# The recurrence's input projection of a two-block transformer: one plain weight slot on raw input, seven slots with seven products each, gates and scan at fixed points

## What is computed

```
x = rmsnorm(x, final_g)                       # end of the first block
h = rms_norm(x, a_norm)                       # a second norm right behind it
proj = h @ w_in                               # 1024 -> 2048
y_branch, x_branch = jnp.split(proj, 2, axis=-1)
gate = gelu(y_branch)                         # tanh form
xc = causal_depthwise_conv(x_branch, conv_w, conv_b)        # 4 taps
r_gate, i_gate = sigmoid(xc by blocks @ w_a + b_a), sigmoid(xc by blocks @ w_x + b_x)
log_a = -8 * r_gate * softplus(-lam)
a, u = exp(log_a), sqrt(-expm1(2 * log_a)) * (i_gate * xc)
h_t = a_t * h_{t-1} + u_t                     # a scan over the 512 positions
x = x + (gate * h) @ w_out                    # the stage called YA
x = x + swiglu(rms_norm(x, a_ffn_norm))       # the stage called SW0
```

## Time and profile before

| | |
|---|---|
| median of 3 runs | 3285.03 us (3284.56 to 3289.19) |
| span of the profiled execution | 3286.2 us |
| PE busy | 3255.1 us, 99% |
| VectorE busy | 2027.2 us, 62% |
| ScalarE busy | 730.0 us, 22% |
| GpSimd busy | 1028.5 us, 31% |
| granted TensorE clock, mean | 0.997 of full speed |

### The profile page before, as it was taken

The page is one execution under the profiler, slowest core; times in us unless marked ns, Lnnn a source line. Parts: engine busy times, 40 slices in busy tenths (PEclk is TensorE's granted clock), DMA queues, the critical chain, the costliest instruction groups (busy, mean ns, idle before and its releaser), DMA issues. The chain is left out here.

```text
span 3286.2 us, 40354 instructions
## 1 busy us (share of the span) xinstructions
PE 3255.1 (99%) x15522; PEld 2464.8 (75%) x15522; DVE 2027.2 (62%) x3686; ACT 730.0 (22%) x1567; POOL 1028.5 (31%) x806
## 2 busy tenths in 40 slices
PE   8999999999999999999999999999999999999999
PEld 6767775555555566788888854888886887888888
DVE  8766777676765624278545656756536688866543
ACT  3432422010101333131111124211101235321111
POOL 0111323323232010224444401444441453344443
PEclk9999999999999999999999999999999999999999
DMA  6434412333331121332222221222223221122222
GB/s 261 138 102 128 126 52 79 114 122 110 119 107 55 61 88 49 97 87 78 90 90 90 80 87 64 80 88 90 90 90 101 81 82 53 40 77 90 90 90 90
DMA packets 66896, 304.51 MB, mean 93 GB/s; under 512 B 8496, under 2 KB 21168, under 8 KB 40720
## 3 DMA queue, kind: packets, MB, share of 16 engines
q1 hardware_dynamic: 54368, 268.68, 24.3%
q0 software_dynamic: 6528, 18.75, 1.8%
q10 hardware_dynamic: 5808, 14.49, 1.3%
HBM read 292.84 MB, written 2.88 MB: 90 GB/s over the span
## 5 line engine op out<-in xcount | busy, mean ns | idle before, releaser
L2857 POOL TENSOR_TENSOR scratch<-ring 128x512 f32<-128x512 f32 (+1 forms) x160 | 217.1, 1357 | 1443.6 <-PE psum L744 952.9
L744 PE MATMUL psum<-big,scratch 128*128 128x256 f32 (+1 forms) x2240 | 606.9, 426 | 0.0
L744 PEld LDWEIGHTS psum<-big,scratch 128*128 128x128 f32 x2240 | 425.6, 190 | 163.7
L744 PE MATMUL psum<-H,scratch 128*128 128x256 f32 (+1 forms) x2144 | 498.9, 387 | 0.0
L744 PEld LDWEIGHTS psum<-H,scratch 128*128 128x128 f32 x2144 | 406.5, 190 | 77.0 <-issue 5.0
L744 PE MATMUL psum<-big,ring 128*128 128x256 f32 (+1 forms) x1584 | 421.4, 418 | 6.6 <-DVE cb L2172 2.5
L744 PE MATMUL psum<-H,ring 128*128 128x256 f32 (+1 forms) x1536 | 396.2, 400 | 1.7 <-issue 0.7
L744 PEld LDWEIGHTS psum<-big,ring 128*128 128x128 f32 x1584 | 300.1, 190 | 111.9 <-DVE cb L2172 3.7
L1480 ACT ACTIVATE cb<-psum 128x256 f32<-128x256 f32 x336 | 129.0, 384 | 1011.0 <-PE psum L744 1011.0
L744 PEld LDWEIGHTS psum<-H,ring 128*128 128x128 f32 x1536 | 290.0, 190 | 76.8 <-ACT H L1578 6.4
L713 PE MATMUL psum<-H,ring 128*128 128x512 f32 x736 | 328.6, 598 | 0.0
(11 more groups left out here) (397 smaller groups left out, 4144.6 us busy)
## 6 DMA issues: line engine op xcount, KB each, us to landing
ring<-in_wall SPq DMA_DIRECT2D x202, 1024.0 KB, 4.9
big<-in_wada SPq DMA_DIRECT2D x48, 512.0 KB, 3.5
big<-in_wada POOLq DMA_DIRECT2D x32, 512.0 KB, 4.1
big<-in_wada SPq DMA_DIRECT2D x8, 1024.0 KB, 21.1
scratch<-in_rpb ACTq DMA_DIRECT2D x16, 512.0 KB, 4.0
big<-big ACTq DMA_DIRECT2D x64, 64.0 KB, 4.9
X<-in_xin SPq DMA_DIRECT2D x4, 768.0 KB, 6.9
scratch<-negd SPq DMA_DIRECT2D x8, 384.0 KB, 9.1
```

What stands on the lines that cost most here:

```text
L744: mm = pe.matmul(fast_bank(st, q, b), lhsT, rhs(k), start=start and k == 0, stop=k == kt - 1, skip_group_check=True)
L2857: pool.tensor_tensor(s1, a21, a22, ALU.add).then_inc(combo_own, 1)
```

## The change

1. The projection's eight plain slots become one plain slot (`raw_slot`) and a fast stage `RX` of seven slots of the new kind `"lru"`.
2. The plain slot's input is `X` times `g_sq` without the roots, written by ScalarE into `GT` as soon as the last MLP has left each tile. The sums of norm 4 (`token_sums`) stand behind its fourth matmul, the spreading of the roots (`spread_roots`) behind its eighth. Its two results are multiplied by the roots afterwards (`scale_first` on VectorE). The filler matmuls of norm 4 are gone (`BRIDGE` has no 4).
3. VectorE makes the input's combinations for `RX` (16 subtractions), interleaved with the first tiles' work, and three additions out of PSUM for each of the seven slots; ScalarE has three more copies and one quarter in each slot. GpSimd makes seven more sets of weight combinations; the first of them starts when slot 101 has landed.
4. The gates, the square roots, the scans, the gelu and the scaling of `X` stand at fixed points of the fast slots, on every engine. The conv's first tap moves from reading PSUM to reading `XB`.
5. The last tiles' gelu stands between the first and second group of `YA`'s input combinations, and in `YA`'s first slot product 2 comes after product 5.
6. `T2` moves to other memory, and a few semaphores are shared, with no other effect on the order.

Of the two functions `branches(x, n)` the first is ScalarE's and the second VectorE's; n is the place in the slot at which it is called.

```diff
-N_UNITS = 2 * 28 + 16 + 12
+N_UNITS = 2 * 28 + 2 + 12
...
+        if self.kind == "lru":
+            return [("lru", 0, s) for s in range(7)]
...
+RX = Stage("lru", False, 101, 72, 4, 0, 40, -1, 2, 8)
...
-                    elif q >= 2:
-                        pe.wait_ge(c21_done, q if rotated else q - 1)
+                    elif q >= 2:
+                        pe.wait_ge(c21_done, q if rotated or at_start(x) else q - 1)
...
-                    late = st.kind == "relu" and slots[x][0] == "out" and slots[x][2] == 0
+                    late = st.kind == "relu" and slots[x][0] == "out" and slots[x][2] == 0 or st is YA and x == 0
...
-            BRIDGE = {1: (3, 11), 2: (3, 12), 3: (3, 8), 4: (8, 5), 6: (4, 4)}
+            BRIDGE = {1: (3, 11), 2: (3, 12), 3: (3, 8), 6: (4, 4)}
...
-            norm(4)
+            def raw_slot():
+
+                r = wait_slot()
+                pe.wait_ge(c11_done, w.fast - 1)
+                pe.wait_ge(c21_done, w.fast - 1)
+                for f in range(2):
+                    for k in range(DT):
+                        if f == 0:
+                            pe.wait_ge(h_ready, 32 + k + 1)
+                        mm = pe.matmul(acc(w.unit), slot_cols(r, k, f * P, P), GT[:, k, :], start=k == 0, stop=k == 7)
+                        if f == 0 and k == 3:
+                            token_sums(4)
+                    mm.then_inc(half_done, 1)
+                    w.unit += 1
+                    if f == 0:
+                        spread_roots(4)
+                w.slot += 1
...
-            for s in range(8):
-                project(xq, normed=32 if s == 0 else None,
-                        after=lambda f, s=s: lru_gates(2 * s + f - 1) if 1 <= 2 * s + f <= DT else None)
-            for p in range(2):
-                pe.wait_ge(acc_free[p], w.unit // 2)
+            gates_at = {(0, 7): 0, (0, 4): 1, (1, 2): 2, (1, 6): 3, (2, 2): 4, (2, 6): 5, (3, 2): 6, (3, 6): 7}
+
+            def between_branches(x, i):
+                if (x, i) in gates_at:
+                    lru_gates(gates_at[x, i])
+
+            fast_stage(RX, between=between_branches)
...
+                    hook(x, 0)
                     copy(q, 5)
                     copy(q, 6)
+                    hook(x, 1)
...
+            def branches(x, n):
+                i = 2 * x + 2
+                y = i - DT
+                if n == 0:
...
+                    else:
+                        gelu_tanh(y - 1)
...
+                def to_branch(q, s):
+
+                    between(s, 0)
+                    took(2, q, c11_done, branch_half(s, 0, 0), 1)
+                    between(s, 1)
+                    took(3, q, c12_done, branch_half(s, 0, 1), 6)
+                    between(s, 2)
+                    took(7, q, c22_done, branch_half(s, 1, 1), 5)
+                    between(s, 3)
...
+            def branches(x, n):     
+
+                i, y = 2 * x + 2, 2 * x - 6
+                if n == 0:
+                    if 1 <= x < 4:
+                        conv(i - 1)
...
+                    if x > 3:
+                        gelu_cube(y - 1)
+                elif n == 1:
...
+                    if x > 3:
+                        lru_scan(y)
+                        gated(y - 1)
+                elif n == 2:
+                    if x > 3:
+                        lru_scan(y + 1)
+                else:
+                    if x < 3:
+                        conv(i)
...
+                    if x >= 3:
+                        gelu_cube(y)
+                    if x == 3:
+                        lru_input(7)
+                        lru_scan(1)
+                    if x in (4, 5):
+                        final_norm(2 * x - 4)
+                        final_norm(2 * x - 3)
+                    if x >= 3:
+                        gated(y)
...
-            pool.wait_ge(lru_v, DT)
+            mix_weights(RX)
             mix_weights(YA)
```

More of the change, by code:

```diff
@@ L287, in build @@
         consts_in = sem("consts_in")
-        x_in = [sem(f"x_in{g}") for g in range(4)]
         bias_in = [sem(f"bias_in{b}") for b in range(4)]
@@ L323, in build @@
         w_in = [sem(f"w_in{b}") for b in range(4)]
-        qw_in = [sem(f"qw_in{b}") for b in range(4)]
+        x_and_qw_in = [sem(f"input_and_query_weights_in{b}") for b in range(4)]
         kv_turned = sem("kv_turned")
@@ L733, in fast_stage, with at_start @@
                 rotated = st is HEADS
+                def at_start(x):
+                    return st is RX and x == 0
                 def product(x, i, b, cols, rhs, start, ready=None):
@@ L779, in first @@
                     elif q >= 2:
-                        pe.wait_ge(c21_done, q if rotated else q - 1)
+                        pe.wait_ge(c21_done, q if rotated or at_start(x) else q - 1)
+                    if st is RX and x == 1:
+                        for p in range(2):
+                            pe.wait_ge(acc_free[p], w.unit // 2)
                     raw, mix = source(x)
@@ L2282, in fast_stage @@
                         to_heads(q0 + x, s)
+                    elif kind == "lru":
+                        to_branch(q0 + x, s)
                     elif kind != "in":
@@ L2723, in gated, with final_norm @@
                 dve.scalar_tensor_tensor(GT[:, i, :], LA[:, i, :], 0.25, GT[:, i, :], ALU.mult, ALU.mult).then_inc(hr_ready, 1)
-            for u in range(2 * DT):
-                if u < DT:
-                    conv(u)
-                else:
-                    gelu_cube(u - DT)
-                if 2 <= u < 2 + DT:
-                    lru_input(u - 2)
-                if u >= DT:
-                    lru_scan(u - DT)
-                if u > DT:
-                    gated(u - DT - 1)
-                if 1 <= u <= DT:
-                    x = X[:, u - 1, CTX:TOK]
-                    own(dve.scalar_tensor_tensor(x, x, v("final_g", u - 1), rstd_s[:], ALU.mult, ALU.mult))
+            def final_norm(k):
+                x = X[:, k, CTX:TOK]
+                own(dve.scalar_tensor_tensor(x, x, v("final_g", k), rstd_s[:], ALU.mult, ALU.mult))
@@ L2739, in _, with gated_tiles @@
+            fast_stage(RX, branches)
+            def gated_tiles(i, j):
+                if j == 0:
+                    dve.wait_ge(prod[(5, 6, 7, 4)[i]], RX.q0 + 7)
+                if i < 2:
+                    dve.wait_ge(hr_ready, 4 * i + j + 1)
+            mix_part(YA, 0, gated_tiles)
+            gelu_cube(DT - 1)
             gated(DT - 1)
-            skip(8, 16)
-            mix_input(YA, lambda h, j: dve.wait_ge(hr_ready, 4 * h + j + 1))
+            for i in (1, 2, 3):
+                mix_part(YA, i, gated_tiles)
```

213 lines of the change are left out of this document (147 added, 66 removed).

## The result

The changed kernel takes 3295.82 us (median of 9 runs, 3293.05 to 3300.01), the kernel before, run beside it, 3287.16 us (9 runs, 3284.56 to 3291.27). The ratio is 1.0026, with a 95% interval of 1.0017 to 1.0034: slower by 8.7 us, where no change was forecast; the time lies above the range of 3276 to 3292. Disturbed runs (5239 to 8733 us, three in all), in which the clock of the whole run was down, are left out of all medians and comparisons here.

What follows compares the result with a forecast made beforehand. TensorE was taken as the bound, busy 3255.1 of 3286.2 us. Terms -14.9 (matmuls) + 10.4 (RX waits) + 1.9 (MLP's last slot) + 2.0 (YA's entry) = -0.6 gave 3284.4 us, range 3276 to 3292.

Steps and rivals of the forecast that it cites:

- a smaller risk: TensorE's clock, outside the sum: waits could bring a fall or two, 2 to 3 us; one fall costs 1.7 us.
- MLP[1]'s last slot: First GpSimd set holds up VectorE's operations ahead of the third addition: 1.9 us more on TensorE's 0.96 us wait.
- The sum of the waits: TensorE's added waiting for VectorE: 10.4 us in RX, 1.9 in MLP[1]'s last slot, 2.0 at YA's entry.
- YA's entry: VectorE's last operations, held up, and the last tile's gelu make TensorE wait: 2.0 us more than the 2.8 before.
- The matmuls taken away: On TensorE: 11.9 us from seven faster slots and 3.0 us from norm 4's fillers, 14.9 us in all.
- The price of a set: Each GpSimd set of four operations holds VectorE up by 2.4 to 3.8 us, taken as 3.1; slot 0 1.9.
- about +4: The whole sum of the change if each set costs VectorE 3.8 us instead of 3.1.
- Case 3: Slower: each collision costs a whole GpSimd operation, 1.23 us, 4.9 a set; +9.1, 3294.1 us. Chance 0.13.
- Its side remark: From slot 4 on, ScalarE's copy stands behind a gelu tanh, so VectorE's lateness reaches products 3 and 7 too.
- Its sign: An RX slot without gates lasting over 15 us would show that whole-operation hold-ups hold.
- case 1: Collisions of VectorE and GpSimd eat the gain: 3284.4 us, own range 3279 to 3291. Chance 0.63.
- The fillers' 3.0 us: At norm 4, filler matmuls of 1.87 + 1.12 us go, their place covered by plain-slot matmuls: 3.0 us gained.

Runs made afterwards that it cites:

- late_and_fillers: Changed kernel with RX's first GpSimd set started after norm 4's last squares, and 29 filler matmuls ahead of waits in slots 2, 4 and YA: 3287.3 us.
- fillers: Changed kernel with filler matmuls to a free bank at four places: MLP's last slot, slots 1 and 4, YA's first slot: 3291.5 us.
- First_set_late: Changed kernel with GpSimd's combinations for the first RX slot started only after norm 4's last squares: 3292.0 us.
- small_sets: Changed kernel with GpSimd's 28 weight combinations for RX's seven slots made over 1 x 4 elements per partition, so left out of the result: 3278.7 us.
- no_fillers_before: Kernel before the change, without norm 4's 13 filler matmuls: 3289.4 us, ratio 1.0003.
- scalar_order: Changed kernel, first set late, with ScalarE's square roots behind slot 2's gates and gelu tanh behind the copies of products 5 and 6: 3290.7 us.
- cube_first: Changed kernel, first set late, with VectorE's gelu cube of each odd tile put ahead of `gated` and, in one slot, a scan: 3293.4 us.
- cube_and_roots: As cube_first, with ScalarE's square roots of four tiles moved from the head of slot 2 to its end: 3290.5 us.
- rebalanced: Changed kernel, first set late, decay squares on ScalarE, square roots at slot 2's end, four final norms moved from slots 4 and 5 to 2 and 3: 3286.5 us.
- rebalanced_fillers: As rebalanced, with 8 fillers ahead of product 3 of slot 4 and 5 ahead of product 5 of YA's first slot: 3285.8 us.

## Why the prediction was wrong

**The step that failed is the clock.** The prediction put it outside the sum, at nothing, as "a smaller risk": "a fall or two, 2 to 3 us". There were five. How long the stretch is with all waits kept and no fall can be read from two kernels: that of late_and_fillers, 184.6, and 2.0 for MLP[1]'s last slot, is 186.6 us; that of fillers, less its 1.8 of misplaced fillers and 1.0 to 1.7 for its one fall, is 186.5 to 187.2. After it is 192.8. So of the 8.7 us the low clock made about 6.2, 1.2 a fall, and the rest, 2.6, is what the sum itself, forecast at -0.6, came to. The medians say the same: 3287.3 + 2.0 against 3295.8 is 6.5 us.

**The sum of the waits: too small in `RX`.** TensorE's idle times after, listed above, come to 17.0 us; before they were 0.96 and 0.52 us at the stretch's ends and 2.8 us at YA's entry. That is 12.7 us more, where the prediction's terms give 10.4 + 1.9 + 2.0 = 14.3. By place:

| term | forecast | idle time measured |
|---|---|---|
| MLP[1]'s last slot | 1.9 | 2.97 - 0.96 = 2.0 |
| slot 0 | 1.5 | 0.43 + 1.24 = 1.7 |
| slot 1 | 0.8 | 0 |
| slots 2 and 3 | 1.5 | 0.29 + 2.02 + 0.28 = 2.6 |
| slot 4 | 3.8 | 3.13 |
| slots 5 and 6 | 2.8 | 0.68 + 1.41 + 1.61 = 3.7 |
| YA's entry | 2.0 | 2.43 - 2.8 = -0.4 |

This looks better than it is. Part of the waiting is hidden by the falls (slot 5: 0.68 us here, 1.43 without falls), and a wait costs more than its idle time in the record: a group of eight matmuls lasts 1.99 us behind one, 1.89 elsewhere. The length of `RX` without a fall has both in it. In late_and_fillers the starts of its first product and of its last product 4 are 2036.25 - 1924.93 = 111.3 us apart; 48 products (12.09 / 7 us each) and eight pairs of gates (1.72) make 96.7. Over by 14.6, where 10.4 was forecast; from there to YA's last product 4 the kernel takes 0.7 us more than before, where 2.0 was forecast. The matmuls taken away, 14.9 us, were rightly priced: -14.9 + 14.6 + 0.7 + 2.0 is 2.4, against 2.6 found.

**Why `RX` was over by 14.6.** The price of a set was too low. First_set_late and small_sets have the same 229 VectorE operations in the stretch, and VectorE is busy for 157.94 us in one and 137.50 in the other. The late first set ran while VectorE was idle; the other six held it up by 20.4 us, 3.4 each (3.8 in slot 4), where the prediction took 1.9 for slot 0 and 3.1 for each of slots 1 to 5, 17.4 in all. With 3.8 its own sum was "about +4". And the budgets had less room than thought: in small_sets, with YA's first set alone beside slot 6, `RX` is over by 2028.89 - 1927.98 - 96.7 = 4.2 us, where 0.7 for slot 4 and 1.4 for slot 6 would make 2.1.

**What was luck.** Case 3 gave 3294.1 us, near what was measured, but its mechanism, a whole GpSimd operation each time and 24.0 us of waits, did not come: a hold-up was 1.1 us at most in these rows. Its side remark did: ScalarE passed VectorE's lateness on to product 3. Its sign, a slot without gates of over 15 us, was no sign: case 1 itself forecasts 12.09 + 3.8 = 15.9 us for slot 4, and late_and_fillers has 15.5 there.

**The fillers' 3.0 us.** no_fillers_before shows that they cost nothing where they stood, so taking them out alone wins nothing. In the changed kernel plain-slot matmuls took their place, as forecast, with no idle time at norm 4, and the 3.0 us were gained; yet one fall came there in the profile.

**Also right:** the stretch as the place of change, the additions out of PSUM unslowed (0.39 to 0.42 us), a wait of 3 to 4 us in RX's fifth slot (3.13), the wait in MLP[1]'s last slot (2.97). **Also wrong:** which operations decide. The prediction summed each slot's work; order tests (scalar_order, cube_first) show that a slot's end is made by the few operations between its additions, and that the sets' place, not only their number, sets the price.

**Open:** how much one fall costs between 1.0 us (2.9 for three in one profiled execution) and 1.7. And whether a fall follows a given wait: 2.42 us brought none in small_sets, 2.43 us one in the changed kernel, 2.02 us none in fillers. The fall behind norm 4's sums is in five of the twelve profiles with this order (after, fillers, cube_and_roots, rebalanced, rebalanced_fillers), four of them without a long wait ahead of it; what decides it is not shown.

## What to carry to other kernels

When a change turns a stretch of pure TensorE work into one that waits, price each wait of 2 us or more twice: itself, and a fall of the clock that may come behind it (here 1.0 to 1.7 us each, five in 200 us). Before a wait that can't be removed, matmuls into a free bank, shorter than the wait, gave 3 to 5 us back and cost no time; the same fillers where nothing waits are a plain cost, so read their places off the timeline. And before reordering a late engine's queue ask what the earlier finish will start: here it let GpSimd's next set begin on the operations that decide.

## What the runs showed of the hardware that was not expected

- The clock falls with TensorE busy in the record. Behind norm 4's sums, 2.6 us of matmuls one column wide with no gap, it was at 0.50 for 3.4 us (1919.50 above); in seven of twelve profiles it was not. The Trainium skill (TensorE: Matmul & The Clock Gate, section "Part 1: The HAM clock gate") ties the clock to how busy TensorE has been; these traces agree for the longest waits (2.97, 2.02, 3.13 and 2.43 us, each with a fall behind it), though not for every one, and show a fall with only narrow matmuls and no idle time right before it.
- A scan is held up too: 2.17 us beside a set in cube_first, 1.22 alone. The Trainium skill (SBUF — State Buffer, section "Who interferes with whom") says so of any VectorE instruction with two inputs in SBUF; here the trace agrees. The hold-up was 0.95 us, where a whole GpSimd operation is 1.27 us.
- GpSimd is held up too, but by less: in the changed kernel's slot 4 three of its four operations of 1.27 us take 1.60 to 1.73, 0.3 to 0.5 us more, while each costs VectorE 0.7 to 1.1 us.
